# One-instruction exponentials in compressed attention, and value products in half tiles, two chunks at a time

## The reference, cut to what matters

```
# compressed branch: 63 block keys per group, all tokens
sc = q @ k_cmp.T * scale - slopes * dist_cmp
p_cmp = masked_softmax(sc, dist_cmp >= 0);  o_cmp = p_cmp @ v_cmp
imp = sum over the group's 4 heads of p_cmp @ overlap   # 16 blocks of 64 keys
sel_idx = top_k(imp + forced, 8)                        # blocks kept per token and group
# selected branch (the 8 blocks) and window branch (256 keys), same queries
p_s = masked_softmax(q @ k_sel.T * scale - slopes * d_sel, ...);  o_s = p_s @ v_sel
p_w = masked_softmax(q @ k_win.T * scale - slopes * d_win, ...);  o_w = p_w @ v_win
o = gate0 * o_cmp + gate1 * o_s + gate2 * o_w
```

## Time and profile before

| | |
|---|---|
| median of 3 runs | 1978.09 us |
| profiled execution: its time, its span | 1977.41 us, 1975.8 us |
| TensorE busy (all of it) | 1798.2 us, 91% of the span |
| end of `prepare_attention` (395 to 439 us) | 44 us, granted clock 0.77 |
| `sparse_attend`, first pairs (439 to 490 us) | 51 us |
| `sparse_attend`, from the fifth pair on (490 to 685 us) | 195 us, granted clock 1.00 |

### The profile page before, as it was taken

One profiled execution on the slowest core, in us unless ns is written; L12 is line 12 of the kernel. 1 busy time (PEld: TensorE's weight loads), 2 busy tenths in 40 slices (PEclk: granted clock), 3 DMA queues, 4 the chain that ended last, 5 costly groups with the idle time before them and its releaser, 6 DMA issues. The chain is left out here.

```text
span 1975.8 us, 27772 instructions
## 1 busy us (share of the span) xinstructions
PE 1798.2 (91%) x10467; PEld 1460.7 (74%) x10468; DVE 1195.1 (60%) x1766; ACT 939.3 (48%) x1288; POOL 321.5 (16%) x260
## 2 busy tenths in 40 slices
PE   8999999768999999799999947999999969999990
PEld 7888888656878878577887736788877748788770
DVE  3324553456655355679989854534344568999884
ACT  5112432453333332368888855323221238888870
POOL 0000000001000001223444300000001133433320
PEclk9999999878999999899999977999999989999995
DMA  5433434501000052589999874111215279999976
GB/s 201 141 123 118 136 119 120 124 34 54 1 1 1 27 200 103 195 339 372 380 372 378 349 256 139 54 42 57 81 54 200 97 288 357 378 375 375 368 287 264
DMA packets 145834, 373.26 MB, mean 189 GB/s; under 512 B 41014, under 2 KB 75966, under 8 KB 120974
## 3 DMA queue, kind: packets, MB, share of 16 engines
q1 hardware_dynamic: 114134, 308.34, 42.9%
q0 software_dynamic: 22368, 45.47, 6.4%
q10 hardware_dynamic: 9216, 17.93, 2.5%
HBM read 330.11 MB, written 75.10 MB: 205 GB/s over the span
## 5 line engine op out<-in xcount | busy, mean ns | idle before, releaser
L1530 PE MATMUL ex_ps_h<-even_split 128*128 128x512 f32 x768 | 194.4, 404 | 7.7 <-DVE even_split L1659 7.5
L1530 PE MATMUL ex_ps_h<-odd_split 128*128 128x512 f32 x768 | 193.0, 401 | 9.1 <-DVE odd_split L1659 7.6
L1530 PEld LDWEIGHTS ex_ps_h<-even_split 128*128 128x128 f32 x768 | 141.7, 191 | 46.3 <-DVE even_split L1659 13.7
L1530 PEld LDWEIGHTS ex_ps_h<-odd_split 128*128 128x128 f32 x768 | 140.4, 189 | 48.0 <-DVE odd_split L1659 13.2
L588 PE MATMUL in_ps<-in_w_hi,in_xT_hi 128*128 128x512 f32 (+1 forms) x440 | 170.3, 387 | 0.6 <-DVE in_xT_lo L466 0.5
L588 PE MATMUL in_ps<-in_w_lo,in_xT_hi 128*128 128x512 f32 (+1 forms) x440 | 167.0, 380 | 0.0
L588 PE MATMUL in_ps<-in_w_hi,in_xT_lo 128*128 128x512 f32 (+1 forms) x440 | 165.4, 376 | 0.0
L1927 PE MATMUL conv_ps<-conv_xT_hi,conv_w_hi 128*128 128x512 f32 x384 | 150.7, 393 | 1.9 <-DVE conv_w_lo L1864 1.9
L1927 PE MATMUL conv_ps<-conv_xT_hi,conv_w_lo 128*128 128x512 f32 x384 | 150.2, 391 | 0.0
L1927 PE MATMUL conv_ps<-conv_xT_lo,conv_w_hi 128*128 128x512 f32 x384 | 150.1, 391 | 0.0
L2668 ACT ACTIVATE att_prob<-att_ps_s 128x512 f32<-128x512 f32 x114 | 67.9, 597 | 154.5 <-PE att_ps_s L2603 154.4
(11 more groups left out here) (371 smaller groups left out, 3998.8 us busy)
## 6 DMA issues: line engine op xcount, KB each, us to landing
all_region<-in_moe_w_gate SPq DMA_DIRECT2D x16, 1024.0 KB, 9.7
all_region<-in_moe_w_up SPq DMA_DIRECT2D x16, 1024.0 KB, 18.5
all_region<-in_moe_w_down SPq DMA_DIRECT2D x16, 1024.0 KB, 13.6
experts_w_gu<-in_moe_w_gate SPq DMA_DIRECT2D x16, 1024.0 KB, 10.1
experts_w_gu<-in_moe_w_up SPq DMA_DIRECT2D x16, 1024.0 KB, 20.8
experts_w_d<-in_moe_w_down SPq DMA_DIRECT2D x16, 1024.0 KB, 15.8
slot_rows<-slots SPq DMA_DIRECT2D x32, 512.0 KB, 6.3
all_region<-in_ev_w_in SPq DMA_DIRECT2D x12, 1024.0 KB, 6.0
```

Source lines behind the costliest of these rows:

```text
L1530: last = pe.matmul(ps_h[:, u % 2, :], a[:, u % 2, k, :], w[:, k, :], start=(k == 0 and j == 0), stop=(k == KT - 1 and j == 2))
```

## The change

In the compressed branch the batches run in the order 2, 3, 0, 1 (index i). The negated maximum is no longer ACT's bias: PE adds it onto the scores in PSUM (`take_maxima_off`, two 128x512 products in fp32r), and ACT exponentiates a whole batch, 128x1024, in one instruction. The sums come from a DVE reduction (`totals`), the shares are no longer divided on DVE; the division is folded into the gate's coefficient. For the two batches that choose, POOL divides and adds over heads (`sum_shares`).

In attention every head's value product becomes two of 64 queries and 65 columns instead of one of 128 queries and 128 columns, and PE takes the chunks two at a time: score i, score i+1, their jobs, then the products of chunks i-2 and i-1. The last two chunks of a pair are weighed after `turn_low`.

```diff
+    order = chooses + [b for b in range(BATCHES) if b not in chooses]
...
+                def sum_shares(i):
+                    p_i = pc[:, i % 2, :, :, :].rearrange("p t h n -> p (t h) n")
+                    pool.wait_ge(totalled, i + 1)
...
+                    pool.tensor_tensor(shares[:].rearrange("p t h n -> p (t h) n"), p_i,
+                                       total[:, i * N:(i + 1) * N].unsqueeze(2).to_broadcast([P, N, NC_]), ALU.mult
+                                       ).then_inc(shared, 1)
...
+                    pool.tensor_tensor(hs_2[:], p_4[:, :, 0:2, :], p_4[:, :, 2:4, :], ALU.add).then_inc(halved, 1)
+                    pool.wait_ge(halved, i + 1)
+                    pool.tensor_tensor(hs[:, i, :, :], hs_2[:, :, 0, :], hs_2[:, :, 1, :], ALU.add).then_inc(heads_summed, 1)
...
-                    for t in range(BATCH):
-                        for h in range(NH):
-                            i = (b * BATCH + t) * NH + h
-                            last = act.activation(pc[:, b % 2, t, h, :], ps_s[b % 2][:, t, h, :], ACT.Exp,
-                                                  bias=less[:, i:i + 1], accum_out=total[:, i:i + 1])
-                    last.then_inc(exped, 1)
+                def exps(i):
+                    act.wait_ge(lowered, i + 1)
+                    if i >= 2:
+                        act.wait_ge(p_turned, (i - 1) * BATCH)
+                        act.wait_ge(totalled, i - 1)
+                        act.wait_ge(shared, min(i - 1, len(chooses)))
+                    act.activation(pc[:, i % 2, :, :, :].rearrange("p t h n -> p (t h n)"),
+                                   ps_s[i % 2].rearrange("p t h n -> p (t h n)"), ACT.Exp).then_inc(exped, 1)
...
+                def totals(i):
+                    s_i = total[:, i * N:(i + 1) * N]
+                    dve.wait_ge(exped, i + 1)
+                    dve.tensor_reduce(s_i, pc[:, i % 2, :, :, :].rearrange("p t h n -> p (t h) n"), X, ALU.add)
...
+                    dve.reciprocal(s_i, s_i).then_inc(totalled, 1)
...
+                totals(0)
+                totals(1)
+                maximum(2)
+                open_gates(0)
+                maximum(3)
+                totals(2)
+                select(0)
+                open_gates(1)
+                totals(3)
+                select(1)
+                open_gates(2)
+                open_gates(3)
...
+                def take_maxima_off(i):
+                    pe_.wait_ge(maxima, i + 1)
+                    for t in range(BATCH):
+                        at = i * N + t * NH
+                        last = pe_.matmul(ps_s[i % 2][:, t, :, :], ident_r[:],
+                                          less[:, at:at + NH].unsqueeze(2).to_broadcast([P, NH, NC_]),
+                                          start=False, stop=True, skip_group_check=True)
+                    last.then_inc(lowered, 1)
...
                     for h in range(R):
 
-                        last = pe.matmul(ps_o[:, b, h * P:(h + 1) * P], prob[:, c % 4, h * P:(h + 1) * P],
-                                         keep.v_all[:, v_at:v_at + P], start=(j == first_tile(t, b) and h == 0), stop=(j == t),
-                                         skip_group_check=True)
+                        for rows in half_queries:
+                            last = pe.matmul(ps_o[rows, b, h * P:h * P + HD + 1], prob[:, c % 4, h * P + rows.start:h * P + rows.stop],
+                                             keep.v_all[:, v_at:v_at + HD + 1], start=(j == first_tile(t, b) and h == 0),
+                                             stop=(j == t), skip_group_check=True)
                     last.then_inc(weighted, 1)
...
                     for i in range(steps):
                         score(n, i)
                         for some in spread(n)[i]:
+                            if some[1] != EXT_ROWS:
+                                job(*some)
+                        if i % 2 == 0 and i + 1 < steps:
+                            continue
+                        for some in ext_rows(n, i):
                             job(*some)
-                        if i:
-                            weigh(n, i - 1)
+                        while weighed < i - 1:
+                            weigh(n, weighed)
+                            weighed += 1
                     if n + 1 < len(pairs):
                         turn_low(n + 1)
-                    weigh(n, steps - 1)
+                    for i in range(weighed, steps):
+                        weigh(n, i)
```

182 lines of the change are left out of this document (97 added, 85 removed).

## The result

The changed kernel takes 1942.37 us (median of 4 runs, 1940.34 to 1943.84) against 1978.12 us of the kernel before in the same comparison: ratio 0.9821, 95% interval 0.9808 to 0.9834, so 36 us faster. A second comparison gave 1942.30 us and 0.9822 (0.9808 to 0.9835). The forecast was 1958.5 with a range down to 1943: right in sign, a little over half of the gain in size (19.6 of 35.8 us), and just outside its range.

What follows compares the result with a forecast made beforehand. TensorE bounds attention, and a chain through ACT's exponentials, DVE and PE ends the preparation. Attention's 14.4 plus the compressed branch's 5.0 gave 19.4 us off 1977.4, 1958.0, stated as 1958.5; eight-in-ten range 1943 to 1978.

Steps and rivals of the forecast that it cites:

- Value products: Attention on PE: two chunks take 1.31 us instead of 1.78; 26.2 us saved over 54 double and 6 single groups.
- Coming out I take 0.10: Attention's value products: 0.10 us charged per group for going from half tiles back to the next full-width score.
- bound of 36: Attention's value products: upper bound of the gain, 36 us, if going in and out of half tiles cost nothing.
- about 35 us: Attention's value products: the same sum, 28.5 us with the price of changing tiles, would be about 35 us without it.
- rival in which the halves do not run side by side: Attention's value products: 0.87 us a chunk, nothing saved, groups still pay; 22 us slower, 2000; chance 0.06.
- What is late next: Attention: a pair's third job waits about 1.2 us for DVE's first reduction; 9.6 us lost, 7.5 in pairs 4 to 13.
- The clock: PE clock in attention: falls behind some of eleven new stalls, costing 4.5 us, between 0 and 18.
- One in four: Attention's eleven new stalls of about 1.2 us: one in four lowers the clock, at 1.65 us each.
- first clock rival: Attention: the clock falls at each of the eleven stalls; 6 us gained, so 1972; chance 0.14.
- falls of twice the length throughout: Attention: clock falls at every stall, staying down twice over or more, eleven times 4.9 us; 30 slower, 2008; chance 0.06.
- The compressed branch: Preparation's end: the chain ends about 430.6 instead of 437.26, 6.7 us; 5 taken, between -2 and 8.
- second rival: Attention: stalls better hidden, no clock drop, going in and out costs half; 33 us gained, 1945; chance 0.12.

Runs made afterwards that it cites:

- two_full: Kernel before with only attention's order changed: chunks two at a time, value products full width with 128 columns, compressed branch as before; 1974.33 us, ratio 0.9981.
- prep_only: Kernel before with only the compressed branch's part of the change, attention as before; 1967.91 us, ratio 0.9955.
- warm_prep: Kernel before with 18 unused 128x512 bf16 matmuls ahead of the compressed branch's first `weigh`; 1977.38 us, ratio 0.9993.
- stall_long: Changed kernel with the first reduction of pairs 5 to 14 done twice on VectorE; 1970.23 us, ratio 0.9956 against the kernel before.
- stall_mid: Changed kernel with an extra 384-element VectorE reduction ahead of the first reduction of pairs 5 to 14; 1957.98 us, ratio 0.9898 against the kernel before.
- halves_one: Kernel before with only the value products in half tiles, old order of one chunk at a time; 1967.70 us, ratio 0.9953.
- att_only: Kernel before with only attention's part of the change, the preparation as before; 1953.58 us, ratio 0.9877.

## Why the prediction was wrong

**Value products: mis-sized.** The step that failed is the price of coming out, "Coming out I take 0.10". It was added to 1.10 us, a row that runs from a load to the first load behind the group and so holds most of the way out already: counted twice. What was left to add is 0.02 us (the next score's second half, 0.34 behind halves and 0.32 behind full products). The rate (1.08 for 32 loads, 1.10 forecast) and the 0.11 for going in (0.09 to 0.10) were near. So a double group saves 0.52 to 0.60 us, in the mean 0.56, and not 0.47; a lone chunk saves the 0.13 of the forecast (0.14). 54 x 0.56 + 6 x 0.14 is 31.1 us against 26.2.

Two more slips: the bound of 36 leaves out the 2.3 us at the pairs' ends, and "about 35 us" without any price of changing should read 41 (54 x 0.68 + 6 x 0.34 + 2.3). The rival in which the halves do not run side by side did not come (0.47 us a chunk, under its mark of 0.80). Its 0.87 us took two passes for an instruction, where a float32 instruction of 512 columns stands 0.24 us ahead of the next (540.78 to 541.02 in the kernel before), which is one pass at 2.4 GHz; so it was priced too high.

**What is late next: right place, too dear.** About 1.2 us of idle was forecast for pairs 4 to 13; the changed kernel shows 0.66 to 1.17. PE's idle in those pairs rose by 6.2 us, from 3.9 to 10.1 (windows from pair 4's `take_low` to pair 14's), and not 7.5. Of the 2.1 us for pairs 0 to 3, 14 and 15 only pair 14's came (0.69); pair 15's is not there (PE is idle 1.7 us from its `take_low` on, before 1.8); and in pairs 0 to 3 the sign was wrong, since there the order brings VectorE its work sooner (`two_full`: 1.3 us less waiting, where 0.5 more was taken).

**The clock: the forecast's worst step.** "One in four" of eleven stalls at 1.65 us was 4.5 us; no fall came, and behind 42 such stalls in four traces none did. It was a rate from four cases, which left out a fifth in the same trace, a gap of 1.73 us at 478 that left the clock alone. Attention before had one fall, at 468, that is gone: some 1.6 us more. The other two traces of the old attention (`prep_only` and `warm_prep`) have one too, in pair 1, and the new order's stalls in pairs 1 to 3 are shorter (1.3 to 1.5 us instead of 1.3 to 1.9), so this may be the order's doing; no run tests it. The price of a fall was right (`stall_long`), the odds at this length were not. The first clock rival (a fall at each stall) describes what happens when the stalls are 1.2 us longer; the second (falls of twice the length throughout, 4.9 us each) was seen nowhere, though two of the ten in `stall_long` and two of the three in `stall_mid` lasted 6.8 us.

**The compressed branch: right.** The rows of the branch are the test here: the chain gave 6.7 us, I took 5, and 6.1 to 6.4 came; shading a worked chain down for a clock that I expected low was wrong. The GpSimd product of 1024 elements, unknown before, takes 1.90 us, under the 3 that were allowed.

**The account.** Attention: 14.4 forecast, 28.9 measured. By stretch, with the forecast's own terms: pairs 4 to 14 had about 14.0 before the clock and gave 18.8 (3.2 of the difference is PE's work, 25.7 us less where 22.5 was forecast, and 1.6 the idle time, 6.9 instead of 8.5); pair 15 had 1.9 and gave 3.1; the start and pairs 0 to 3 had about 2.9 and gave 6.9 (1.0 of it the start, 1.6 the old fall of the clock); the clock had -4.5 and gave nothing. What came is in substance the second rival (stalls hidden better, no fall, 1945), which had a chance of 0.12: of the 0.21 us that it put on top of the row's 1.10, 0.12 was left, about half. Nearly all errors had one sign, as each unknown was taken a little against the change.

## What to carry to other kernels

Half-width tiles pay off only with few changes of tile: here 0.28 us a group against 0.42 us saved a chunk, so grouping two chunks doubled what a chunk gains (0.14 to 0.28 us), and the next thing to move is whatever that grouping has left waiting. Work that holds up another engine goes behind work that only this engine needs: the same instructions, with jobs behind the products, gave another 10 to 12 us. A rate taken from a row that runs to the next instruction's start holds most of the way out; do not add it again.

Before a stretch of two traces is compared, look for falls of the clock in it: here single ones, with a cost of 1.6 to 2.6 us each, sat in the old kernel, in `halves_one` and in `att_only`, and looked like gains or losses of the change.

## What the runs showed of the hardware

- Eight float32 products at full width take 0.81 us up to a float32 score, with 65 moving columns as with 128, and 0.84 against 0.89 up to a bf16 mask: the moving columns do not set their pace. In halves, two 64-column loads side by side, it is 29 ns an instruction (0.47 us for 16).
- A group of halves between full-width work costs 0.28 us in the mean (0.42 saved per chunk, 0.14 for a lone one), 0.10 of it on the way in; price and saving are worked out from busy times and not read from one row.
- The same stall (1.66 to 2.17 us) was followed by 1.2 GHz three times in seven; in another run ten of ten from 1.69 to 2.83 us were, and none of 42 from 0.66 to 1.17 us in four traces. Ten falls cost 1.8 us each beside the stall itself. Some 0.5 us of VectorE work added in ten places cost 16 us, and 0.9 us cost 28.
- A multiply of 128 x 16 on VectorE that runs beside GpSimd's product of 1024 elements took 1.93 us once, and 0.18 to 0.35 elsewhere in that trace; in `prep_only` one took 0.93. It was not on the chain that ended last as far as the trace shows; I did not test it.

```profile
403.77 1.90 POOL L2148 TENSOR_TENSOR prep_shares<-prep_pc,prep_total 128x1024 f32<-128x1024 f32 x1 [29.11 <-DVE prep_total L2294]
403.77 1.93 DVE L2297 TENSOR_TENSOR prep_coef<-prep_total,mix_gate 128x16 f32<-128x16 f32 x1
```
